# Feed-forward operands: the parts of the second quarter ahead of the last quarter's scaling and of the second difference

## The chip, the cores and the metric

The kernel runs on one core of a Trainium2 chip. The metric is the device time of one execution in microseconds, lower is better. Engines: TensorE (PE in the profile) multiplies, VectorE (DVE), ScalarE (ACT) and GpSimd (POOL) work elementwise, SyncE (SP) issues DMAs; ScalarE issues some too. Each takes its instructions from its own queue in program order and waits on semaphores that the others increment.

## The reference

One layer of a hybrid decoder over 2048 prompt tokens and 32 sample tokens, all fp32. The part that matters here is the feed-forward and the embedding that the kernel computes ahead of it:

```python
def hybrid_layer(x, pe, ...):
    ...
    x = x + jnp.concatenate([h_m, y_c], axis=-1) @ w_out
    f = rmsnorm(x, g_ffn)
    x = x + (jax.nn.silu(f @ w_gate) * (f @ w_up)) @ w_down
    e = rmsnorm(pe @ w_ple, g_ple)
    x = x + jax.nn.sigmoid(x @ w_pg) * e
```

The model width is 1024, the hidden width 2816. Ahead of this lie the input projection, an mLSTM with a recurrent state, and a short convolution.

## The kernel before

**Groups and stages.** Tokens are handled in three groups q of 704 (the last of 672, with the sample tokens). Each goes through the stages in, out, the embedding (ple), feed-forward (ffn) and pg, with all weights read anew. Activations lie with features on partitions; a group is cut into two halves of 352 (336) columns.

**Products.** A weight block of 1024 x 256 is multiplied as a 2 x 2 by 2 x 2 block product in Winograd's form, with 7 products in place of 8. Each of these runs over 4 blocks of 128 rows. fp32 accuracy comes from a split: every operand is held as a high part, rounded to fp32r, and a low part, the rest; `three` issues hi x hi, hi x lo and lo x hi. So a product is 12 matmuls of 352 columns. The order here is P1, P5, P2, P6, P7, P4, P3 (`FIRST_PRODUCTS`), and in feed-forward the first gate pair and the first up pair run as twins: P1 of gate, P1 of up, P5 of gate, P5 of up, and so on. These 14 products have the slots s = 0 to 13; hooks called `ffn_first` (one on ScalarE, one on VectorE) run behind slot s.

**Operands.** The moving operands of the stage are seven, made once for all pairs. With f the normed input, B11, B21 the upper and lower features of the first half, B12, B22 of the second:

- operand 0 is B11 (`R45`), read by P1; operand 4 is T1 = B12 - B11 (`mixq`), read by P5
- operand 1 is B21 (`mixr`), the second quarter, read by P2
- operand 2 is B22 (`qraw[:, 2]`), the last quarter, read by P3; it is made by a scaling with the norm's factors, `f_normed(q, 1, 1, ...)`
- operand 5 is the second difference T2 = B22 - T1 (`R67`), made by `t_sums(q, "ffn", 5)`, read by P6
- operand 6 is T2 - B11 (P7), operand 3 is B21 - T2 (P4), made by `t_sums` with 6 and 3

ScalarE makes the high part of an operand with one copy (`high_of`, line 1301), which waits until the operand is made. VectorE subtracts it from the operand for the low part (`low_of`, line 1778) and waits for the copy. For operand 2 GpSimd does that (its own `low_of`, line 2666), and waits for operand 5 to be made besides.

**Who does what around the twin pair.** `embedding` on each engine runs while TensorE multiplies the embedding: 16 small products k, each evicted by ScalarE (line 1540). VectorE makes operands 0, 4, 1, 2 and 5 there. In the twin pair each engine calls `product` per slot, and ahead of its own work `ahead()`, which prepares one weight entry further on: ScalarE rounds it (line 1283) and GpSimd subtracts (line 2652), for the entry four products ahead; VectorE forms the weight sums S1 to S4. In the second and third group most entries are loaded from DRAM instead, where the first group stored them; ScalarE issues these loads in `ahead()`. An entry lies in one of five ring slots and may be overwritten once its product is done.

On ScalarE a slot is `ahead()`, then for P1 and P2 the eviction of the bank, then the hook. On VectorE a slot is `ahead()`, then the sum that takes in the bank of this product (line 1889 for P6, lines 1894 and 1897 or 1899 to 1904 for P7, 1911 for up's P2), then the hook. P6 and P7 of a pair use the same bank, so P7 starts only when line 1889 is done.

SyncE loads the raw weights of a block (`raw`) as soon as the last weight entry of the block two before has its low part, in one of two buffers `wraw`.

In the table of counters the low parts are waited for in this order, one semaphore for 0 to 6 and another (`low2`) for operand 2:

```python
def highs(q, st):
    ...
    return 0, 4, 1, 5, 6, 3, 2
```

Of the kernel before, what the change touches and what calls it, by code (L numbers as in the profile page):

```python
# [58 lines left out]
def sources(q, st):  # L59

    if st == "in":
        return 0, 1, B12, 2, 4, 5, 3, 6
    return {"out": (0, 4, 5, 6, 3), "ffn": (0, 4, 1, 2, 5, 6, 3), "pg": (4, 5, 6, 3)}[st]


def highs(q, st):

    if st == "in":
        return (0, B12, 1, 2, 4, 5, 3, 6) if q else (0, 1, B12, 2, 4, 5, 3, 6)
    return 0, 4, 1, 5, 6, 3, 2  # L70


def slot(i):

    return 6 if i == B12 else i
# [90 lines left out]
def build(nc, x_prompt, x_sample, p_prompt, p_sample, state_C, state_n, state_m, state_conv, g_mix, w_in,  # L166
# [129 lines left out]
    def source(q, st, i):  # L296
        if i in (3, 6) or st == "pg" and i == 5:
            return qraw[:, i, :, 0:q.N]
        c = q.blocks
        if st in ("in", "out"):  # L300
            a = q.A if st == "in" else q.U
            if i == 5:
                return qraw[:, 5, :, 0:q.N] if st == "in" else Rz[:, :, 0:q.N]
            return {0: a[:, 0:4, c[0]], B12: a[:, 0:4, c[1]], 4: a[:, 0:4, c[1]], 1: a[:, 4:8, c[0]], 2: a[:, 4:8, c[1]]}[i]
        if st == "ffn":
            return {0: R45, 4: mixq, 1: mixr, 2: qraw[:, 2], 5: R67}[i][:, :, 0:q.N]
        return {0: q.X[:, 0:4, c[0]], 1: q.X[:, 4:8, c[0]], 2: q.X[:, 4:8, c[1]], 4: diff[:, :, 0:q.N]}[i]
# [190 lines left out]
    def freed(q, st, i):  # L498

        if st == "in" and i == 6:  # L500
            return operand_end[(q, "in", B12)]
        if st == "in" and q == 0:
            return None
        return operand_end[(q - (st == "in"), BEFORE[st], slot(i))]

    with ExitStack() as ctx:
# [744 lines left out]
        def _(act):  # L1251
# [33 lines left out]
            def ahead():  # L1285

                one_ahead()
                if n_hi[0] < len(entries) and entries[n_hi[0]].spare is not None:
                    one_ahead()

            def high_of(q, st, i):

                if i in sources(q.n, st):
                    act.wait_ge(src_ready, SOURCE[(q.n, st, i)])
                elif st == "out":
                    act.wait_ge(gated, 6 * q.n + (5 if i == 1 else 6))
                else:
                    act.wait_ge(x3, 16 * q.n + (7, 15, 16)[i])
                if freed(q.n, st, i):
                    act.wait_ge(prod, freed(q.n, st, i))  # L1300
                nc.scalar.activation(qhi[:, slot(i), :, 0:q.N], source(q, st, i), ACT.Copy).then_inc(high, 1)
# [228 lines left out]
                return after  # L1530

            def embedding(q):
                for k in range(16):
                    if k % 4 == 0:
                        ahead()
                    if k == 1:
                        res_square(q, 3)
                    act.wait_ge(*written[(q.n, "ple", k)])
                    bk = 6 + k % 2
                    nc.scalar.activation(q.U[:, k // 2, q.blocks[k % 2]], bank[bk][:, 0:q.N], ACT.Copy).then_inc(free[bk], 1)  # L1540
                    if k in (10, 13):
                        high_of(q, "ffn", {10: 0, 13: 4}[k])
# [22 lines left out]
            def silu_part(q, c, b, name):  # L1565
                act.wait_ge(*drained[(q.n, "gate", 0, name)])
                nc.scalar.activation(sl[:, c, q.blocks[b]], sl[:, c, q.blocks[b]], ACT.Silu).then_inc(silu_done, 1)

            def ffn_first(q):
                def after(s):  # L1570
                    if s in (0, 2, 4, 6, 8):
                        high_of(q, "ffn", highs(q.n, "ffn")[2 + s // 2])
                    if s == 8:
                        silu_part(q, 1, 1, "P5")
                    if s == 10:
                        silu_part(q, 1, 0, "P4")
                    if s == 12:
                        silu_part(q, 0, 1, "P3")
                    if s == 13:
                        hidden_high(q, 0, 1)  # L1580
                return after
# [56 lines left out]
            q = supers[0]  # L1638
# [65 lines left out]
            q = supers[2]  # L1704
# [5 lines left out]
        def _(dve):  # L1710
# [65 lines left out]
            def low_of(q, st, i):  # L1776
                dve.wait_ge(high, HIGH[(q.n, st, i)])
                nc.vector.tensor_tensor(qlo[:, slot(i), :, 0:q.N], source(q, st, i), qhi[:, slot(i), :, 0:q.N], sub)\  # L1778
                    .then_inc(low2 if i == 2 else low, 1)

            def made(q, st, *which):

                dve.wait_ge(src_ready, max(SOURCE[(q.n, st, i)] for i in which))

            def free_operand(q, st, i):
                if freed(q.n, st, i):
                    dve.wait_ge(prod, freed(q.n, st, i))
# [572 lines left out]
            def embedding(q):  # L2360
                for k in range(3):
                    ahead()
                    if k == 0:
                        res_add(q, 3)
                mean_squares(q, "res", 5, res_mean, 2 * (q.n + 1))
                f_normed(q, 0, 0, R45).then_inc(src_ready, 1)
                link(f_normed(q, 0, 1, mixq))
                made(q, "ffn", 0)
                nc.vector.tensor_tensor(mixq[:, :, 0:q.N], mixq[:, :, 0:q.N], R45[:, :, 0:q.N], sub).then_inc(src_ready, 1)
                low_of(q, "ffn", 0)  # L2370
                ahead()
                f_normed(q, 1, 0, mixr).then_inc(src_ready, 1)
                made(q, "ffn", 1)
                dve.sem_inc(free[3], 1)
                low_of(q, "ffn", 4)
                free_operand(q, "ffn", 2)
                f_normed(q, 1, 1, qraw[:, 2]).then_inc(src_ready, 1)
                made(q, "ffn", 2)
                dve.sem_inc(free[4], 1)
                t_sums(q, "ffn", 5)  # L2380
# [29 lines left out]

            def ffn_first(q):
                def after(s):
                    if s in (0, 2, 4, 6):
                        low_of(q, "ffn", (1, 5, 6, 3)[s // 2])
                    if s in (0, 2):
                        t_sums(q, "ffn", (6, 3)[s // 2])
                    if s == 13:
                        hidden_low(q, 0, 1)
                return after
# [115 lines left out]
            q = supers[0]  # L2535
# [63 lines left out]
            q = supers[2]  # L2599
# [8 lines left out]
        def _(pool):  # L2608
# [52 lines left out]
            def low_of(q, st):  # L2661

                pool.wait_ge(high, HIGH[(q.n, st, 2)])
                if st == "ffn":
                    pool.wait_ge(src_ready, SOURCE[(q.n, "ffn", 5)])
                nc.gpsimd.tensor_tensor(qlo[:, 2, :, 0:q.N], source(q, st, 2), qhi[:, 2, :, 0:q.N], ALU.subtract).then_inc(low2, 1)
# [147 lines left out]
            for q in supers:  # L2814
                plain_pair(q, in_after(q))
                ahead()
                ahead()
                for i in range(1, IN_PAIRS):
                    pair(in_after(q), 7 * i)
                for j in range(14):  # L2820
                    ahead()
                    if j == 8:
                        low_of(q, "out")
                for i in range(2, 4):
                    pair(nothing, 0)
                for k in range(4):
                    ahead()
                    if k == 1:
                        inverse_means(q, res_mean, res_root)
                for p in range(FFP):  # L2830
                    if p == 0:
                        for j in range(14):
                            ahead()
                            if j == 9:
                                low_of(q, "ffn")
                        continue
                    pair(nothing, 0)
                    if down_before(p) is not None:
                        for k in range(8 if down_before(p) else 4):
                            ahead()  # L2840
                    if p == 1:
                        for k in range(5):
                            ahead()
                        inverse_means(q, e_mean, e_root)
                        ahead()
                        ahead()
                    else:
                        pair(nothing, 0)
                for k in range(8):
                    ahead()  # L2850
                for i in range(4):
                    pair(pg_after(q), 7 * i)

            q = supers[2]
# [28 lines left out]
```

## Time and profile before

| | |
|---|---|
| median of 3 runs | 2640.02 us (2639.51 to 2642.21) |
| the profiled execution | 2641.59 us, its span 2639.9 us |
| TensorE busy | 2504.7 us, 95% of the span |
| VectorE busy | 1487.6 us, 56% |
| GpSimd busy | 1054.5 us, 40% |
| ScalarE busy | 908.1 us, 34% |
| mean granted clock of TensorE | 0.978 of full |

The profile is of one execution. Busy times are sums over instructions; a gap of TensorE is read in its timeline, where the bracket says how long it stood idle and which instruction ended that. "issue" there means that no releaser shows. Line numbers are those of the kernel before. The three groups' feed-forward starts lie at about 368, 1250 and 2103 us.

### The profile page before, as it was taken

Reading aid. Unit: us, or ns where it says so; the run is one execution under the profiler, and the core shown is the slowest. Engines: PE = TensorE matmul, PEld = TensorE weight load, DVE = VectorE, ACT = ScalarE, POOL = GpSimd, SP = SyncE. Lnnn points to the kernel's source line nnn. Section 1 sums busy time; section 2 is a strip of 40 time slices with the busy share of each in tenths; the row PEclk is TensorE's granted clock in tenths of the full one; section 3 lists DMA queues with packets and bytes.
Section 4 is the critical chain, followed back from the end, with each engine's and each line's share of the span. In section 5 each row is a group of like instructions: output and inputs, shape, how many; then the busy total and the mean of one; then the engine's idle time right before and its main releaser. Section 6 shows DMA issues by size and latency. Waiting matters only on the chain.

```text
span 2639.9 us, 41288 instructions
## 1 busy us (share of the span) xinstructions
PE 2504.7 (95%) x15883; PEld 2442.7 (93%) x15883; DVE 1487.6 (56%) x2283; ACT 908.1 (34%) x1687; POOL 1054.5 (40%) x864
## 2 busy tenths in 40 slices
PE   7998888999999999999999999998999999999997
PEld 6898778999999988999999999998899999999997
DVE  6667877765555674466643333467347664333355
ACT  5344443343333542333322121354134432212133
POOL 4566645676666343222332122334223232312233
PEclk8999888999999999999999999999999999999999
DMA  5556635576566746565555545575557555564544
GB/s 185 201 182 225 213 113 178 205 267 218 201 224 236 232 143 193 175 230 176 188 172 200 171 150 174 176 236 161 182 173 230 189 195 167 192 200 160 174 146 162
DMA packets 285046, 501.04 MB, mean 190 GB/s; under 512 B 18427, under 2 KB 182612, under 8 KB 284342
## 3 DMA queue, kind: packets, MB, share of 16 engines
q1 hardware_dynamic: 212182, 273.59, 30.8%
q10 hardware_dynamic: 72672, 224.82, 26.0%
q8 instruction: 129, 2.11, 0.3%
q14 instruction: 63, 0.52, 0.1%
HBM read 374.70 MB, written 123.65 MB: 189 GB/s over the span
## 4 chain that ended last, share of the span: by engine, by line
PE 69%; DVE 8%; DMA 6%; issue 3%; POOL 3%; ACT 1%; DVEq 0%; POOLq 0%; ACTq 0%
PE bank L603 22%; PE bank L605 21%; PE bank L604 21%; POOL wring L2652 3%; DMA wring<-weight_parts 2%; DMA weight_parts<-wring 2%; DVE qlo L1778 1%; PE bank L726 1%; DMA xs<-x_prompt 1%; PE bank L737 1%; DVE sg L2513 0%; PE bank L789 0%; PE bank L795 0%; ACT wring L1283 0%; DVE wraw L1768 0%
## 5 line engine op out<-in xcount | busy, mean ns | idle before, releaser
L2652 POOL TENSOR_TENSOR wring<-wraw,wring 128x512 fp32r<-128x512 f32 x531 | 785.3, 1488 | 1232.8 <-ACT wring L1283 1230.0
L603 PE MATMUL bank<-qhi,wring 128*128 128x352 f32 (+1 forms) x3588 | 1175.6, 328 | 72.7 <-DVE u L1832 14.9
L605 PE MATMUL bank<-qhi,wring 128*128 128x352 f32 (+1 forms) x3588 | 1157.2, 323 | 0.0
L604 PE MATMUL bank<-qlo,wring 128*128 128x352 f32 (+1 forms) x3588 | 1156.3, 322 | 0.0
L603 PEld LDWEIGHTS bank<-qhi,wring 128*128 128x128 f32 x3588 | 684.9, 191 | 98.9 <-issue 80.6
L604 PEld LDWEIGHTS bank<-qlo,wring 128*128 128x128 f32 x3588 | 684.5, 191 | 0.0
L605 PEld LDWEIGHTS bank<-qhi,wring 128*128 128x128 f32 x3588 | 682.3, 190 | 0.0
L1283 ACT ACTIVATE wring<-wraw 128x512 fp32r<-128x512 f32 x531 | 331.4, 628 | 734.8 <-PE bank L605 549.1
L603 PE MATMUL bank<-hid,wring 128*128 128x352 f32 (+1 forms) x1056 | 340.5, 322 | 11.2 <-DVE wide L2472 6.1
L605 PE MATMUL bank<-hid,wring 128*128 128x352 f32 (+1 forms) x1056 | 339.3, 321 | 0.0
L604 PE MATMUL bank<-hid,wring 128*128 128x352 f32 (+1 forms) x1056 | 338.4, 320 | 0.0
L2472 DVE TENSOR_TENSOR wide<-wide,bank 128x352 f32<-128x352 f32 (+1 forms) x288 | 148.1, 515 | 293.1 <-PE bank L605 293.1
L603 PEld LDWEIGHTS bank<-hid,wring 128*128 128x128 f32 x1056 | 199.5, 189 | 15.2 <-issue 11.6
L604 PEld LDWEIGHTS bank<-hid,wring 128*128 128x128 f32 x1056 | 200.1, 189 | 0.0
L605 PEld LDWEIGHTS bank<-hid,wring 128*128 128x128 f32 x1056 | 199.3, 189 | 0.0
L1839 DVE TENSOR_TENSOR u<-t,bank 128x352 f32<-128x352 f32 (+1 forms) x84 | 43.2, 514 | 189.0 <-PE bank L605 188.9
L2652 POOL TENSOR_TENSOR wring<-s,wring 128x512 fp32r<-128x512 f32 x74 | 107.8, 1468 | 69.0 <-ACT wring L1283 68.5
L1832 DVE TENSOR_TENSOR u<-t,bank 128x352 f32<-128x352 f32 (+1 forms) x87 | 44.6, 512 | 139.5 <-PE bank L605 110.9
L1563 ACT ACTIVATE hid<-sl 128x704 fp32r<-128x704 f32 (+3 forms) x69 | 52.1, 755 | 186.6 <-DVE sl L1810 181.0
L2406 DVE TENSOR_TENSOR hid<-sl,hid 128x704 fp32r<-128x704 f32 (+3 forms) x69 | 102.5, 1496 | 9.2 <-ACT hid L1563 7.5
L1312 ACT ACTIVATE t<-bank 128x352 f32<-128x352 f32 (+1 forms) x123 | 56.3, 457 | 135.9 <-PE bank L605 135.7
L1283 ACT ACTIVATE wring<-s 128x512 fp32r<-128x512 f32 x74 | 45.7, 628 | 91.2 <-PE bank L605 52.3
(318 smaller groups left out, 2468.7 us busy)
## 6 DMA issues: line engine op xcount, KB each, us to landing
wring<-weight_parts ACTq DMA_DIRECT2D x418, 512.0 KB, 4.5
weight_parts<-wring SPq DMA_DIRECT2D x201, 512.0 KB, 3.9
wraw<-w_down SPq DMA_DIRECT2D x33, 1024.0 KB, 7.1
wraw<-w_in SPq DMA_DIRECT2D x14, 1024.0 KB, 6.7
wraw<-w_gate SPq DMA_DIRECT2D x11, 1024.0 KB, 6.0
wraw<-w_up SPq DMA_DIRECT2D x11, 1024.0 KB, 6.1
wraw<-w_in SPq DMA_DIRECT2D x44, 256.0 KB, 4.3
wraw<-w_gate SPq DMA_DIRECT2D x44, 256.0 KB, 4.2
```

What stands on the lines that cost most here:

```text
L603: nc.tensor.matmul(o, hi, mh, start=begins, stop=False, skip_group_check=True)
L604: nc.tensor.matmul(o, hi, ml, start=False, stop=False, skip_group_check=True)
L605: return nc.tensor.matmul(o, lo, mh, start=False, stop=ends, skip_group_check=True)
L726: last = nc.tensor.transpose(bank[bk][0:n, c * P:(c + 1) * P], q.X[:, m * 4 + c, t0:t0 + n], ident[:, :])
L1283: nc.scalar.activation(whi[e % RING][:, :].rearrange("p (k n) -> p k n", k=k), w.src, ACT.Copy).then_inc(hi_done, 1)
L1312: nc.scalar.activation(t1[n % 2][:, 0:q.N], bank[a][:, 0:q.N], ACT.Copy).then_inc(free[a], 1)
L1563: nc.scalar.activation(hid[:, 0, x, blk], sl[:, c, blk], ACT.Copy).then_inc(h_hi, 1)
L1832: nc.vector.tensor_tensor(w2, t, c, add).then_inc(fc, 1)
L1839: nc.vector.tensor_tensor(w3, w2 if first else t, d, add).then_inc(fd, 1)
L2406: nc.vector.tensor_tensor(hid[:, 1, x, blk], sl[:, c, blk], hid[:, 0, x, blk], sub).then_inc(h_lo, 1)
L2472: last = nc.vector.tensor_tensor(x, x, bank[bk][:, 0:q.N], add)
L2652: nc.gpsimd.tensor_tensor(wlo[e % RING][:, :].rearrange(v, k=k), w.src, whi[e % RING][:, :].rearrange(v, k=k), ALU.subtract).then_inc(lo_d ...
```

## The change

On ScalarE the copy for the high part of operand 1 moves from the hook of slot 0 to the end of `embedding`, behind its last eviction, and the copies of operands 5, 6, 3 and 2 move from slots 2, 4, 6, 8 to 0, 2, 4, 6. On VectorE the low part of operand 1 moves from slot 0 to `embedding`, ahead of the scaling that makes operand 2 and of the second difference; the low parts of 5, 6 and 3 move from slots 2, 4, 6 to 0, 2, 4. The sums that make operands 6 and 3 keep their slots 0 and 2, behind the low part in the same slot. On GpSimd the low part of operand 2 moves from behind the tenth to behind the eighth weight entry of the twin pair.

```diff
             def embedding(q):
-                for k in range(16):
+                for k in range(17):
+                    if k == 16:
+                        high_of(q, "ffn", 1)
+                        break
                     if k % 4 == 0:
                         ahead()
...
             def ffn_first(q):
                 def after(s):
-                    if s in (0, 2, 4, 6, 8):
-                        high_of(q, "ffn", highs(q.n, "ffn")[2 + s // 2])
+                    if s in (0, 2, 4, 6):
+                        high_of(q, "ffn", highs(q.n, "ffn")[3 + s // 2])
...
                 low_of(q, "ffn", 4)
+                low_of(q, "ffn", 1)
                 free_operand(q, "ffn", 2)
                 f_normed(q, 1, 1, qraw[:, 2]).then_inc(src_ready, 1)
...
             def ffn_first(q):
                 def after(s):
-                    if s in (0, 2, 4, 6):
-                        low_of(q, "ffn", (1, 5, 6, 3)[s // 2])
+                    if s in (0, 2, 4):
+                        low_of(q, "ffn", (5, 6, 3)[s // 2])
                     if s in (0, 2):
                         t_sums(q, "ffn", (6, 3)[s // 2])
...
                         for j in range(14):
                             ahead()
-                            if j == 9:
+                            if j == 7:
                                 low_of(q, "ffn")
```

## Rows read from the trace of the kernel before

**Rows 1.** View by stretches, the three twin pairs: busy us (xcount) by engine

```profile
368.50:408.80 40.30, 32.11 (x170) 31.07 (x169) 36.07 (x35) 18.00 (x27) 23.59 (x14) 0.87 0.43 157
1250.20:1277.90 27.70, 27.04 (x168) 26.50 (x167) 21.77 (x24) 14.19 (x19) 12.35 (x5) 1.00 0.64 226
2103.10:2129.70 26.60, 25.97 (x170) 25.71 (x169) 21.05 (x25) 13.77 (x20) 11.99 (x5) 1.00 0.66 230
```

**Rows 2.** TensorE's timeline at its gaps: start, us, instruction, [idle before <-releaser]

```profile
379.32 0.63 PE L603 MATMUL bank<-qhi,wring 128*128 128x352 f32 x1 [2.47 <-issue]
...
393.77 0.63 PE L603 MATMUL bank<-qhi,wring 128*128 128x352 f32 x1 [5.01 <-DVE u L1889]
...
404.91 0.40 PE L603 MATMUL bank<-qhi,wring 128*128 128x352 f32 x1 [0.52 <-issue]
...
418.48 0.63 PE L603 MATMUL bank<-qhi,wring 128*128 128x352 f32 x1 [3.79 <-DVE u L1832]
...
1258.39 0.40 PE L603 MATMUL bank<-qhi,wring 128*128 128x352 f32 x1 [0.55 <-issue]
...
2110.97 0.39 PE L603 MATMUL bank<-qhi,wring 128*128 128x336 f32 x1 [0.63 <-issue]
```

**Rows 3.** Timeline of VectorE, second group

```profile
1248.09 2.05 DVE L2356 SCALAR_TENSOR_TENSOR mixr<-wide,gains,bank 128x352 f32<-128x352 f32 x4
...
1254.02 1.62 DVE L2008 TENSOR_TENSOR R<-qraw,mixq 128x1408 f32<-128x1408 f32 x1
1255.56 2.72 DVE L1778 TENSOR_TENSOR qlo<-mixr,qhi 128x1408 fp32r<-128x1408 f32 x1
1258.21 1.61 DVE L2012 TENSOR_TENSOR qraw<-R,R 128x1408 f32<-128x1408 f32 x1
...
1264.79 0.51 DVE L1889 TENSOR_TENSOR u<-t,bank 128x352 f32<-128x352 f32 x1
1265.22 1.85 DVE L1778 TENSOR_TENSOR qlo<-qraw,qhi 128x1408 fp32r<-128x1408 f32 x1
```

**Rows 4.** Timeline of ScalarE, second group

```profile
1249.91 0.81 ACT L1540 ACTIVATE wide<-bank 128x352 f32<-128x352 f32 x2
...
1252.48 1.38 ACT L1301 ACTIVATE qhi<-mixr 128x1408 fp32r<-128x1408 f32 x1
1253.75 0.63 ACT L1283 ACTIVATE wring<-wraw 128x512 fp32r<-128x512 f32 x1
...
1254.27 0.46 ACT L1312 ACTIVATE t<-bank 128x352 f32<-128x352 f32 x1
1255.68 1.38 ACT L1301 ACTIVATE qhi<-R 128x1408 fp32r<-128x1408 f32 x1 [0.95 <-DVE R L2008]
```

**Rows 5.** Timeline of VectorE, first group

```profile
374.81 2.27 DVE L2008 TENSOR_TENSOR R<-qraw,mixq 128x1408 f32<-128x1408 f32 x1
...
393.12 0.51 DVE L1889 TENSOR_TENSOR u<-t,bank 128x352 f32<-128x352 f32 x1
...
400.17 1.55 DVE L1752 TENSOR_TENSOR s<-wraw 128x512 f32<-128x512 f32 x1 [1.42 <-DMA wraw<-w_gate]
```

**Rows 6.** Timeline of GpSimd, first and second group

```profile
386.82 7.50 POOL L2652 TENSOR_TENSOR wring<-wraw,wring 128x512 fp32r<-128x512 f32 x4 [1.10 <-ACT wring L1283]
...
401.12 3.69 POOL L2666 TENSOR_TENSOR qlo<-qraw,qhi 128x1408 fp32r<-128x1408 f32 x1
...
1254.45 2.35 POOL L2652 TENSOR_TENSOR wring<-wraw,wring 128x512 fp32r<-128x512 f32 x1 [1.38 <-ACT wring L1283]
```

**Rows 7.** Timeline of SyncE's queue, first group

```profile
394.35 0.38 SPq L1069 DMA_DIRECT2D wraw<-w_gate  x1
```

**Rows 8.** The page's DMA issues: KB each, median us to landing

```profile
wring<-weight_parts ACTq DMA_DIRECT2D x418, 512.0 KB, 4.5
```

**Rows 9.** View by stretches, behind gaps of 1.81 and 1.77 us

```profile
1295.00:1303.00 8.00, 7.73 (x48) 7.73 (x49) 4.21 (x9) 0.00 (x0) 0.00 (x0) 1.00 0.53 142
2147.00:2152.00 5.00, 5.00 (x24) 4.99 (x24) 1.57 (x4) 0.00 (x0) 0.00 (x0) 0.66 0.52 152
```

## The prediction

> **What bounds the kernel now.** I first cut the run into stretches and took the three feed-forward starts, one per group of tokens [rows 1]. TensorE is busy for 27.04 of 27.70 us in the second group and 25.97 of 26.60 in the third, at full clock; in the first group only for 32.11 of 40.30, clock 0.87. So TensorE sets the pace and what I look for are its gaps. Its own timeline then gives them [rows 2]: in the first group 2.47 us ahead of P2 of the gate (at 379.32; it needs the low part of operand 1), 5.01 ahead of P7 (at 393.77; released by VectorE's line 1889, the sum that empties the bank of P6), 0.52 ahead of P3 (404.91; operand 2's low part) and 3.79 in the next pair. In the second and third group the only gap up to the end of the twin pair is that ahead of P2: 0.55 and 0.63 us. VectorE's timeline of the second group [rows 3] shows why: it works through one list without a pause. ScalarE's timeline [rows 4] shows the rounding copies (line 1301) between its own evictions and weight preparations.
>
> **What the order of the code does to the queues.** I write low(i) and high(i) for the parts of operand i, s for the slot after each product. ScalarE executes slot s of the twin pair as: prepare the weights of product s+4, evict, then the hook. Each hook's high(i) waits until operand i is made, and everything behind it in ScalarE's queue waits too. Before, high(1) sits in slot 0 and is ready at once; high(5) in slot 2 (1252.48 and 1255.68 [rows 4]). After, high(5) moves to slot 0, high(6) to slot 2, high(3) to slot 4, high(2) to slot 6. On VectorE low(1) goes ahead of the scaling of operand 2 and of T2, and low(5), low(6), low(3) each move two slots forward. Nothing is added or removed: the same copies, subtractions and loads. But two couplings change. First, low(3) (1.85 us at 1265.22) ran behind the sum of line 1889 (1264.79) and now runs ahead of it. Second, VectorE had always another subtraction between making an operand and needing its high part back: T2 made, then low(1) and T6, and only then low(5) [rows 3]. After, the order is T2, low(5), T6, low(6), T3, low(3): each low part needs a copy by ScalarE that can't start before the operation just ahead of it on VectorE. The copy of 1.38 us is no longer covered, three times over.
>
> **The second group, step by step.** mixr is made at 1250.14 (1248.09 plus 2.05); ScalarE has finished its two evictions at 1250.7, so high(1) runs 1250.6 to 1252.0 and low(1) 1252.0 to 1253.6 at the 1.62 of an undisturbed subtraction. Scaling of operand 2 (2.05) and T2 (1.62, with 0.14 between as now) end at 1257.45 instead of 1255.64: +1.8. From there, each subtraction by its spacing (four of them and the short sum of line 1911, 0.44, fill 1258.21 to 1264.79: 1.54 each; 1.6 behind a wait) and each copy by 1.38 with 0.05 of hand-over: high(5) to 1258.9, low(5) 1260.5, T6 1262.05, high(6) 1263.5, low(6) 1265.1, T3 1266.65, high(3) 1268.1, low(3) 1269.7, the up pair's P2 sum 1270.1, line 1889 1270.6. P7 of the gate starts 0.14 later (393.12 plus 0.51 against 393.77 in the first group [rows 2, 5]): 1270.75. It started four products behind P2 of the gate: 1258.39 + 48 matmuls of 0.16 (27.04 us for 168 [rows 1]) = 1266.1. So +4.65 where no subtraction is disturbed.
> A subtraction of VectorE beside one of GpSimd took 2.72 instead of 1.62 (low(1) at 1255.56 [rows 3] beside the weight's low part at 1254.45, which took 2.35 [rows 6]). Up to three of the list can meet one (weights of P2, of up P2, of P4): 0 to 3.3 more. I take 1.0, as GpSimd is on in 12.35 of 27.7 us [rows 1] and in some meetings it is GpSimd that gets longer: +5.6 in all, between 4.0 and 8.
> The Trainium skill (SBUF — State Buffer, section Who interferes with whom) says that a VectorE operation with two SBUF inputs and a GpSimd operation that reads SBUF take turns, the second one waiting until the first is done. The trace's 2.72 agrees. By that rule in full, three meetings of a whole GpSimd subtraction would make the step some 8; without it, 4.65.
> What the early low(1) gives: P2 of the gate starts without its 0.55. But the up pair's P2 then waits: its weights are prepared and the bank of its P1 evicted (1253.75 and 1254.27 [rows 4]) behind high(5) now, thus at 1259 to 1260, and GpSimd's low part (1.3 to 2.4 us) ends near 1261.7, where it began at 1260.3. P6 and P6 of up wait likewise, for weights whose loads ScalarE issues only behind high(5) and high(6); a load lands 4.5 us after its issue in the median [rows 8]. Near 1264.5 and 1268.2 they start, against 1262.3 and 1264.2. All of this ends at about 1270.2, still ahead of line 1889, so it adds nothing: it is cover, and would take over if the list were shorter. Behind P7 nothing is early enough to be pinned elsewhere: sums, bank releases and the loads behind the Silu all follow P7, so the delay stays to the end.
>
> **The third group** is the same with 336 for 352 columns, so every term times 0.954: P7, which started at 2110.97 + 48 matmuls of 0.154 = 2118.4 [rows 1, 2], comes 4.4 later, with 0.95 for meetings 5.3, between 3.7 and 7.6.
>
> **The first group** also forms weight sums on VectorE. T2 ended at 377.08 [rows 5]; with low(1) ahead near 378.3. The sums S3 are now covered by waits for high(6), S4 is not. With the medium length of each subtraction I get low(5) 381.9, T6 383.7, high(6) 385.1, low(6) 387.6, T3 389.2, high(3) 390.6, low(3) 392.8, S4 of the gate 394.5, line 1889 396.7: P7 +3 (0.8 to 5.5). In exchange P2 of the gate starts 2.47 earlier, which up P2 gives back waiting for weights until about 381.8. Then the queue of GpSimd: its low(2) (3.69 us, at 401.12 [rows 6]) moves from slot 9 to slot 7, ahead of the weight of slot 8, the last of this gate's raw matrix. That weight's low part ended at 394.3, when SP issued the load of the next w_gate (394.35 [rows 7]), and VectorE's first sum of it began when it landed, at 400.17 [rows 5]. After: high(2) near 393, the weights of slots 5 to 7 to 396, low(2) to 399.7, slot 8 to 401.3, the load to 407. That is +6.7 for a list on VectorE that runs from 400.17 to the release at 418.48 [rows 2, 5]. With fewer meetings behind it I take +6.0, between 3 and 8; the 0.52 ahead of P3 goes, within it.
>
> **The clock.** A gap of 1.77 us in the third group is followed by a stretch at 0.66 of full clock over 5 us, i.e. the lower level of 1.2 GHz for 3.4 of them: 1.7 lost. After a gap of 1.81 us in the second group it stays at 1.00 [rows 9]. The second and third group get four gaps of 6 us in sum within 13 us. Where P7 and what follows run at the lower level, 1.5 to 1.7 is lost; I take 1.2 for each, between 0 and 1.7.
>
> **Sum.** 6.0 + 5.6 + 5.3 + 2.4 = 19.3 us. Against the profiled run of 2641.6 this is 2660.9; that run is 1.6 above the median, so 2659.3.
>
> **Rivals.** (a) The early operand keeps its worth: the three gaps ahead of P2 go (2.47 + 0.55 + 0.63), and the lower clock behind the first (about 1.4), with the 0.52 of P3: 5.6 faster, 2634.4. This needs line 1889 done by 1265.5 in the second group, thus the list from T2 in 8 us; four subtractions alone take 6.5, and three copies would have to be hidden. Against it speaks that each copy reads what was made just before. (b) The delay of P7 comes, but is taken up later: the 3.79 of the next pair in the first group and gaps of 1.8 in each of the others (1295.27 is one) absorb it. 19.3 less 7.4 is 11.9: 2651.9. Against it: those gaps too end with VectorE, which is late as well. (c) Only the operands' order counts and GpSimd's move is hidden: first group +3, 2656.3. (d) The lower clock covers most of the twin pair in the second and third group and meetings come thrice: 8 + 7.6 + 3.4 + 8, 27 slower: 2667. (e) It does nothing measurable, since TensorE waits elsewhere: nothing in the profile speaks for it.
>
> **How the numbers follow.** My case with (c), within 2651 to 2666: 7 in 10. (b): 0.14. (d): 0.09. (a): 0.04, (e): 0.03. The range goes from 2648 (all low ends: 3 + 4.0 + 3.7, less 2 for some of (b)) to 2667 and leaves out less than 2 in 10. Within 0.2% (5.3 us) of before, about what a measurement of this kernel can tell from no change, lies only (e): 0.03. Faster by more than that is (a): 0.04. Slower is the rest, 0.93.
>
> **What would show it.** In the profile after: ScalarE's copy of R (operand 5) directly ahead of the weight preparation that up P2 waits for; VectorE with three idle times of about 1.4 us ahead of line 1778, released by ScalarE; low(3) ahead of line 1889; the gap ahead of P7 in all three groups, released by line 1889, and P7 about 3, 5.6 and 5.3 later; the w_gate load of the first group issued near 401. I would be wrong if ScalarE's copies were found under other work of VectorE, or if TensorE's gaps from the following pair on shrank by what P7 was late.

## The result and the profile after

The changed kernel takes 2657.82 us (median of 5 runs, 2655.41 to 2661.39) against 2640.02 of before: ratio 1.0063, with an interval from 1.0051 to 1.0074. Slower by 17.8 us, clear of the noise. The forecast was 2659.3, from 2648 to 2667.

To see where, I measure each group between two marks that VectorE sets: its scaling of the means ahead of the feed-forward (line 2346 before, 2349 after) and the same line for the embedding's means, behind the second pair. Before, the three stretches are 109.95, 86.00 and 84.36 us; after, 116.07, 92.07 and 90.11. That is 6.1 + 6.1 + 5.8 = 17.9 us, all of the difference. In the page of the profile, TensorE has no more work than before (2498.8 us against 2504.7, and the same number of instructions), while the span has grown by 17.7:

```profile
span 2657.6 us, 41288 instructions
...
PE 2498.8 (94%) x15883; PEld 2434.8 (92%) x15883; DVE 1490.6 (56%) x2283; ACT 907.4 (34%) x1687; POOL 1054.4 (40%) x864
```

TensorE's timeline at its gaps, to be read beside [rows 2]:

```profile
380.67 0.57 PE L603 MATMUL bank<-qhi,wring 128*128 128x352 f32 x1 [3.41 <-POOL wring L2656]
...
396.66 0.63 PE L603 MATMUL bank<-qhi,wring 128*128 128x352 f32 x1 [8.43 <-DVE u L1892]
...
409.92 0.40 PE L603 MATMUL bank<-qhi,wring 128*128 128x352 f32 x1 [1.31 <-DVE bank L1903]
...
424.42 0.63 PE L603 MATMUL bank<-qhi,wring 128*128 128x352 f32 x1 [5.44 <-DVE u L1835]
...
1266.30 0.43 PE L603 MATMUL bank<-qhi,wring 128*128 128x352 f32 x1 [1.86 <-POOL wring L2656]
...
1271.52 0.43 PE L603 MATMUL bank<-qhi,wring 128*128 128x352 f32 x1 [1.13 <-DMA wring<-weight_parts]
...
1276.41 0.40 PE L603 MATMUL bank<-qhi,wring 128*128 128x352 f32 x1 [2.71 <-DVE u L1892]
...
1286.54 0.43 PE L603 MATMUL bank<-qhi,wring 128*128 128x352 f32 x1 [0.35 <-DMA wring<-weight_parts]
...
2126.79 0.42 PE L603 MATMUL bank<-qhi,wring 128*128 128x336 f32 x1 [1.86 <-POOL wring L2656]
...
2131.78 0.42 PE L603 MATMUL bank<-qhi,wring 128*128 128x336 f32 x1 [1.03 <-DMA wring<-weight_parts]
...
2136.50 0.39 PE L603 MATMUL bank<-qhi,wring 128*128 128x336 f32 x1 [2.60 <-DVE u L1892]
...
2147.32 0.42 PE L603 MATMUL bank<-qhi,wring 128*128 128x336 f32 x1 [1.37 <-DMA wring<-weight_parts]
```

The gap ahead of P2 of the gate is gone in all groups. Up P2 now waits (1.86 us in the second and third group, 3.41 in the first) for a weight's low part. Up P6 waits for a load (1.13 in the second group, 1.03 in the third). P7 waits for line 1892 (1889 before): 2.71 in the second group, 2.60 in the third and 8.43 in the first, in place of 0, 0 and 5.01. In the first group the 0.52 ahead of P3 of the gate is gone, but up P3 now waits 1.31 for a sum of VectorE (the row at 409.92). VectorE's timeline of the second group shows why, in place of [rows 3]:

```profile
1252.80 2.05 DVE L2359 SCALAR_TENSOR_TENSOR mixr<-wide,gains,bank 128x352 f32<-128x352 f32 x4
...
1256.69 1.62 DVE L1781 TENSOR_TENSOR qlo<-mixr,qhi 128x1408 fp32r<-128x1408 f32 x1
...
1260.43 1.62 DVE L2011 TENSOR_TENSOR R<-qraw,mixq 128x1408 f32<-128x1408 f32 x1
1263.50 1.62 DVE L1781 TENSOR_TENSOR qlo<-R,qhi 128x1408 fp32r<-128x1408 f32 x1 [1.45 <-ACT qhi L1301]
1265.04 2.68 DVE L2015 TENSOR_TENSOR qraw<-R,R 128x1408 f32<-128x1408 f32 x1
1269.17 1.62 DVE L1781 TENSOR_TENSOR qlo<-qraw,qhi 128x1408 fp32r<-128x1408 f32 x1 [1.45 <-ACT qhi L1301]
1270.72 1.62 DVE L2019 TENSOR_TENSOR qraw<-mixr,R 128x1408 f32<-128x1408 f32 x1
1273.78 1.62 DVE L1781 TENSOR_TENSOR qlo<-qraw,qhi 128x1408 fp32r<-128x1408 f32 x1 [1.45 <-ACT qhi L1301]
...
1275.75 0.95 DVE L1892 TENSOR_TENSOR u<-t,bank 128x352 f32<-128x352 f32 x2
```

Where there was no pause there are three of 1.45 us, each released by ScalarE's line 1301, and low(3), the row at 1273.78, is ahead of the sums of line 1892 (two rows merged at 1275.75). ScalarE, in place of [rows 4]:

```profile
1255.27 1.39 ACT L1301 ACTIVATE qhi<-mixr 128x1408 fp32r<-128x1408 f32 x1
...
1262.09 1.38 ACT L1301 ACTIVATE qhi<-R 128x1408 fp32r<-128x1408 f32 x1 [4.56 <-DVE R L2011]
...
1263.38 0.61 ACT L1283 ACTIVATE wring<-wraw 128x512 fp32r<-128x512 f32 x1
1263.89 0.45 ACT L1312 ACTIVATE t<-bank 128x352 f32<-128x352 f32 x1
1267.76 1.38 ACT L1301 ACTIVATE qhi<-qraw 128x1408 fp32r<-128x1408 f32 x1 [3.42 <-DVE qraw L2015]
...
1272.37 1.38 ACT L1301 ACTIVATE qhi<-qraw 128x1408 fp32r<-128x1408 f32 x1 [1.45 <-DVE qraw L2019]
```

ScalarE stands idle for 4.56 us until T2 is made, copies operand 5 (1262.09), and only then comes to the weight preparation (1263.38) and the eviction (1263.89) that up P2 needs.

The first group, by GpSimd, SyncE and VectorE, in place of [rows 5 to 7]:

```profile
397.17 3.20 POOL L2670 TENSOR_TENSOR qlo<-qraw,qhi 128x1408 fp32r<-128x1408 f32 x1
400.33 1.28 POOL L2656 TENSOR_TENSOR wring<-wraw,wring 128x512 fp32r<-128x512 f32 x1
```

```profile
401.63 0.38 SPq L1069 DMA_DIRECT2D wraw<-w_gate  x1
```

```profile
408.08 0.69 DVE L1755 TENSOR_TENSOR s<-wraw 128x512 f32<-128x512 f32 x1 [6.46 <-DMA wraw<-w_gate]
```

low(2) runs at 397.17, ahead of the weight at 400.33; only then is w_gate issued, at 401.63, and VectorE stands idle for 6.46 us until it lands. Counted from the marks (352.35 and 352.74), the load is issued 49.3 us in, where it was 41.6 before.

### The profile page after: what moved, and what is told of

Read it like the earlier page. It is cut to its first block, busy times and chain, and to the rows that moved or that the text cites. A ratio compares the mean times of both kernels' runs of the same rounds, so it can differ in the third digit from the quotient of the medians.

```text
span 2657.6 us, 41288 instructions
## 1 busy us (share of the span) xinstructions
PE 2498.8 (94%) x15883; PEld 2434.8 (92%) x15883; DVE 1490.6 (56%) x2283; ACT 907.4 (34%) x1687; POOL 1054.4 (40%) x864
## 4 chain that ended last, share of the span: by engine, by line
PE 65%; DVE 9%; DMA 7%; POOL 4%; issue 4%; ACT 2%; DVEq 0%; POOLq 0%; ACTq 0%; SPq 0%
PE bank L603 20%; PE bank L605 20%; PE bank L604 20%; POOL wring L2656 3%; DMA weight_parts<-wring 3%; DMA wring<-weight_parts 2%; DVE qlo L1781 1%; ACT qhi L1301 1%; PE bank L726 1%; PE bank L737 1%; DVE sg L2517 0%; PE bank L789 0%; ACT wring L1283 0%; DVE ess L2393 0%; DMA xs<-x_prompt 0%
## 5 line engine op out<-in xcount | busy, mean ns | idle before, releaser
L603 PEld LDWEIGHTS bank<-hid,wring 128*128 128x128 f32 x1056 | 198.9, 188 | 16.3 <-issue 12.5
```

The source lines that it names most:

```text
L603: nc.tensor.matmul(o, hi, mh, start=begins, stop=False, skip_group_check=True)
```

## The experiments

All times are medians, with the ratio to the kernel before that ran on the same chip. Beside these experiments single executions of the kernel before went from 2632 to 2647 us, so a difference of a few us between two experiments is weak by the medians; the stretches and gaps of the profiles show more. A profile is of one execution, though, and that one can lie far from its median: e6's is the slowest of its runs, e4's, e8's and e10's are among the fastest. The column "profiled" gives its time. The last column is TensorE's time lost to the lower clock in the second and third stretch (1 less the granted clock, times the time, summed over pieces of 2 us). The first stretch loses 10 to 16 us in every profile (13.3 before, 14.2 changed).

| kernel | median us | ratio (interval) | profiled | 1st stretch | 2nd | 3rd | lost 2nd, 3rd |
|---|---|---|---|---|---|---|---|
| before | 2640.0 | 1 | 2641.6 | 109.95 | 86.00 | 84.36 | 0, 1.7 |
| changed | 2657.8 | 1.0063 (1.0051 to 1.0074) | 2659.3 | 116.07 | 92.07 | 90.11 | 0, 0 |
| e1 early only | 2639.7 | 0.9994 (0.9984 to 1.0004) | 2640.0 | 110.44 | 87.29 | 84.52 | 1.7, 1.7 |
| e2 GpSimd back | 2658.7 | 1.0073 (1.0055 to 1.0091) | 2660.5 | 115.82 | 93.14 | 89.74 | 3.4, 1.7 |
| e3 low(3) back | 2655.0 | 1.0051 (1.0036 to 1.0067) | 2654.2 | 116.65 | 91.07 | 87.42 | 0, 1.7 |
| e4 copies covered | 2651.9 | 1.0045 (1.0031 to 1.0058) | 2646.2 | 114.68 | 89.46 | 86.42 | 1.7, 1.7 |
| e5 shift only | 2660.4 | 1.0082 (1.0064 to 1.0099) | 2659.8 | 115.08 | 92.68 | 89.92 | 3.4, 3.4 |
| e6 ScalarE a slot later | 2657.8 | 1.0069 (1.0049 to 1.0089) | 2667.9 | 115.01 | 94.52 | 90.57 | 5.1, 3.4 |
| e7 low(3) back, covered | 2655.2 | 1.0057 (1.0040 to 1.0074) | 2658.0 | 114.10 | 91.52 | 87.51 | 3.4, 1.7 |
| e8 every repair | 2641.0 | 1.0003 (0.9990 to 1.0016) | 2636.0 | 109.44 | 88.06 | 82.60 | 1.7, 0 |
| e9 e8, low(3) ahead | 2645.7 | 1.0022 (1.0013 to 1.0031) | 2645.7 | 109.62 | 89.79 | 83.61 | 1.7, 0 |
| e10 e8, copies open | 2649.8 | 1.0035 (1.0021 to 1.0049) | 2644.2 | 110.45 | 88.40 | 86.74 | 0, 0 |
| e11 e8, GpSimd early | 2647.5 | 1.0023 (1.0011 to 1.0034) | 2642.2 | 112.67 | 86.15 | 83.22 | 0, 0 |

**Is it the early operand or the shift of the others?** e1 keeps the first and undoes the second; e5 does the reverse.

```diff
# e1, against the changed kernel
-                    if s in (0, 2, 4, 6):
-                        high_of(q, "ffn", highs(q.n, "ffn")[3 + s // 2])
+                    if s in (2, 4, 6, 8):
+                        high_of(q, "ffn", highs(q.n, "ffn")[2 + s // 2])
...
-                    if s in (0, 2, 4):
-                        low_of(q, "ffn", (5, 6, 3)[s // 2])
+                    if s in (2, 4, 6):
+                        low_of(q, "ffn", (5, 6, 3)[s // 2 - 1])
...
-                            if j == 7:
+                            if j == 9:
```

> Against the changed kernel, only the early copy and subtraction of operand 1 stay; operands 5, 6, 3, 2 and GpSimd's subtraction return to their old slots. Theory of the prediction (the cost comes from the two-slot shift, not from the early operand): low(3) is again behind the sum that frees P6's bank and each copy of ScalarE is covered by another operation of VectorE, so P7 is on time; the gap ahead of gate P2 goes. 2638.5 us, between 2636 and 2641. Rival (the early low part itself costs, since T2 ends 1.8 us later in each group): 1 to 2 us slower per group than before, 2643 to 2646.

Measured 2639.7, ratio 0.9994: no different from before. The early operand costs nothing; it doesn't bring anything either. The gap ahead of gate P2 is gone in all groups, but in the first group TensorE then stands for 4.51 us ahead of gate P6 (the row below), since VectorE's list is no shorter; in the third it waits 0.50 us for a load right behind the twin pair.

```profile
387.68 0.40 PE L603 MATMUL bank<-qhi,wring 128*128 128x352 f32 x1 [4.51 <-issue]
```

```diff
# e5, against the changed kernel
-                for k in range(17):
-                    if k == 16:
-                        high_of(q, "ffn", 1)
-                        break
+                for k in range(16):
...
             def ffn_first(q):
                 def after(s):
+                    if s == 0:
+                        high_of(q, "ffn", 1)
                     if s in (0, 2, 4, 6):
...
-                low_of(q, "ffn", 1)
                 free_operand(q, "ffn", 2)
...
             def ffn_first(q):
                 def after(s):
+                    if s == 0:
+                        low_of(q, "ffn", 1)
                     if s in (0, 2, 4):
```

> The changed kernel with operand 1's copy and subtraction back in slot 0 (low(1) ahead of low(5)), the two-slot shift of 5, 6, 3 and 2 kept. Theory: T2 ends 1.8 us earlier, low(1) covers the copy of operand 5, and of the three idle times of VectorE two stay, as does low(3) ahead of the sum that frees P6's bank: P7 3.9 and 3.7 us later than before in the second and third group, some 4.6 in the first: 2652, between 2649 and 2655. Rival 1 (the early low(1) is what costs): 2640 to 2643. Rival 2 (the early low(1) costs nothing, all comes from the shift): 2657.

Measured 2660.4, ratio 1.0082, above the expected range: rival 2 by the time. In the second group P7 (the row below) starts 33.10 us behind the mark; before it was 1266.1 - 1236.94 = 29.2. So it is 3.9 late, as worked out, not 5.6. The rest of these two stretches is clock: this profile loses 3.4 us in the second and third each, the changed kernel's none. In the first group P7 is only 2.1 late, and the stretch 5.1 longer: w_gate lands 7.0 later from the mark than before. The shift alone makes the whole loss, though not by P7's delay alone.

```profile
1272.29 0.63 PE L603 MATMUL bank<-qhi,wring 128*128 128x352 f32 x1 [2.84 <-DVE u L1891]
```

**Which coupling of the shift?** e3 moves low(3) back behind the sum, e4 covers two copies, e6 takes ScalarE's copies off up P2's weights.

```diff
# e3, against the changed kernel
-                    if s in (0, 2, 4):
-                        low_of(q, "ffn", (5, 6, 3)[s // 2])
+                    if s in (0, 2, 6):
+                        low_of(q, "ffn", {0: 5, 2: 6, 6: 3}[s])
```

> The changed kernel with VectorE's low(3) alone back in slot 6, behind the sum that frees P6's bank. Theory: P7 of the gate comes earlier by low(3) and the idle time ahead of it, 1.54 + 1.45 = 3.0 us in each group; in the second and third group that stays to the end; in the first it does not, since the load of w_gate waits for GpSimd's queue (weights of slots 5 to 7, then low(2)), which starts from the copy of operand 3 and is not moved. So 6 us less than the changed kernel: 2652. Rival 1 (the place of low(3) is the whole cost): 5.6 less per group, near 2641. Rival 2 (copies without cover are the whole cost and low(3) is not): 2657.

Measured 2655.0, 2.9 less than the changed kernel where 6 were worked out; by the times alone rival 2 is not excluded (the intervals overlap), the stretches give 1.0 and 2.7 less in the second and third group. In the first group nothing is gained, as expected. The next fence is TensorE's timeline of e3 in the second group: no wait for line 1892 is left ahead of P7, but four of the weight path are, two of them new, ahead of up P7 and right behind the twin pair.

```profile
1266.73 0.43 PE L603 MATMUL bank<-qhi,wring 128*128 128x352 f32 x1 [1.94 <-POOL wring L2656]
...
1271.84 0.43 PE L603 MATMUL bank<-qhi,wring 128*128 128x352 f32 x1 [0.99 <-DMA wring<-weight_parts]
...
1276.58 0.43 PE L603 MATMUL bank<-qhi,wring 128*128 128x352 f32 x1 [0.65 <-DMA wring<-weight_parts]
...
1287.80 0.43 PE L603 MATMUL bank<-qhi,wring 128*128 128x352 f32 x1 [1.29 <-DMA wring<-weight_parts]
```

```diff
# e4, against the changed kernel
-                    if s in (0, 2, 4):
-                        low_of(q, "ffn", (5, 6, 3)[s // 2])
                     if s in (0, 2):
                         t_sums(q, "ffn", (6, 3)[s // 2])
+                    if s in (0, 2, 4):
+                        low_of(q, "ffn", (5, 6, 3)[s // 2])
```

> The changed kernel with VectorE's order inside slots 0 and 2 turned round: T6 ahead of low(5), T3 ahead of low(6), so that ScalarE's copies of 5 and 6 lie under a subtraction. low(3) stays ahead of the sum that frees P6's bank. Theory: the three idle times of VectorE (1.45 each) go, the list ends 4.3 us earlier; TensorE is then held by up P2's weights and starts P7 near 4.1 us earlier than in the changed kernel in the second and third group, 3 in the first: 2646.5, between 2644 and 2650. Rival (the place of low(3) is what costs): no more than 1 us less than the changed kernel, 2656 to 2658.

Measured 2651.9 (2645.6 to 2655.0), 6 less than the changed kernel where 11 were worked out. P7 waits for no sum in the second and third group. The stretches, of a profiled run at 2646.2, gain 1.4, 2.6 and 3.7. The open copies are thus a part of the cost, and by these figures a larger one than low(3) (e9 and e10 below show each alone); the rival is out.

```diff
# e6, against the changed kernel
-                    if s in (0, 2, 4, 6):
+                    if s in (1, 3, 5, 7):
                         high_of(q, "ffn", highs(q.n, "ffn")[3 + s // 2])
```

> The changed kernel with ScalarE's copies of 5, 6, 3, 2 one slot later (1, 3, 5, 7), thus behind the eviction and the weight preparation that up P2 waits for. Theory: up P2, P6 and up P6 start earlier, their gaps go, the gap ahead of P7 grows by as much, the time stays: 2657.8, within 1.5. Rival (the late weights of up P2, P6 and up P6, 1.9 + 1.1 us per group of gaps, are the cost): 3 us less per group, 2649.

Measured 2657.8, as expected, no different from the changed kernel. The gaps of up P2 and up P6 are gone in the second group, and the one ahead of P7 has nearly their sum (5.29 us, for 1.86 + 1.13 + 2.71; first fence: TensorE's timeline of e6). P7 did start a little earlier from the mark, by 0.7 to 0.9 us in each group, but this profile, of the slowest run (2667.9), lost 8.5 us to the clock in the second and third stretch. The second fence is its view by stretches behind that gap.

```profile
1277.95 0.63 PE L603 MATMUL bank<-qhi,wring 128*128 128x352 f32 x1 [5.29 <-DVE u L1892]
```

```profile
1277.90:1283.90 6.00, 5.95 (x23) 5.99 (x24) 1.38 (x3) 0.50 (x1) 4.55 (x3) 0.57 0.71 196
```

e7 joins e3 and e4: both repairs of VectorE's list, with ScalarE's order and GpSimd's left as in the changed kernel.

```diff
# e7, against the changed kernel
-                    if s in (0, 2, 4):
-                        low_of(q, "ffn", (5, 6, 3)[s // 2])
                     if s in (0, 2):
                         t_sums(q, "ffn", (6, 3)[s // 2])
+                    if s in (0, 2, 6):
+                        low_of(q, "ffn", {0: 5, 2: 6, 6: 3}[s])
```

> The changed kernel with both repairs of VectorE's order: T6 ahead of low(5), T3 ahead of low(6), and low(3) behind the sum that frees P6's bank. ScalarE's order and GpSimd's stay. Theory: VectorE no longer holds P7 in the second and third group; what stays is the wait of up P2 for weights behind the copy of operand 5 (2.0 us, against the 0.55 of before), thus +1.5 to 2 per group, and in the first group GpSimd's queue ahead of the w_gate load, +3: 2646, between 2643 and 2649.

Measured 2655.2, far more than expected. No gap for line 1892 is left in the second and third group; the wait of up P2 is (2.06 us in each), and loads that up P3 waits for add 0.40 and 1.05. Right behind the wait of up P2 the lower clock takes 1.7 more, 1.6 of it in the row below (view by stretches of e7, from the gap at 1266.34 on):

```profile
1266.00:1270.40 4.40, 4.06 (x16) 4.07 (x17) 3.82 (x3) 3.44 (x5) 0.43 (x2) 0.64 0.92 313
```

**Everything repaired, and then each cost by itself.**

```diff
# e8, against e7
-                    if s in (0, 2, 4, 6):
+                    if s in (1, 3, 5, 7):
                         high_of(q, "ffn", highs(q.n, "ffn")[3 + s // 2])
...
-                            if j == 7:
+                            if j == 8:
```

> As the run before, and ScalarE's copies of 5, 6, 3, 2 one slot later (1, 3, 5, 7) so that up P2's weights are not behind them, and GpSimd's low(2) behind the ninth weight, so that it is ahead neither of the last weight of the gate matrix nor behind the Silu. Theory: every cost found is gone, the gap ahead of gate P2 too; no gap above 0.5 us up to P7 in the second and third group; first group as before or 1 us shorter. 2638, between 2635 and 2640.5. Rival (moving these parts at all costs, by meetings of VectorE and GpSimd): 2643 or more.

Measured 2641.0, ratio 1.0003, just above the expected range. All of the loss is undone, and nothing is won. VectorE's list in the second group of e8 has no pause, as before the change (first fence). TensorE waits 0.59 us for a load ahead of up P3 instead (second fence):

```profile
1246.88 1.77 DVE L2011 TENSOR_TENSOR R<-qraw,mixq 128x1408 f32<-128x1408 f32 x1
1248.76 1.62 DVE L2015 TENSOR_TENSOR qraw<-R,R 128x1408 f32<-128x1408 f32 x1
1250.30 1.62 DVE L1781 TENSOR_TENSOR qlo<-R,qhi 128x1408 fp32r<-128x1408 f32 x1
1251.84 1.62 DVE L2019 TENSOR_TENSOR qraw<-mixr,R 128x1408 f32<-128x1408 f32 x1
1253.38 1.62 DVE L1781 TENSOR_TENSOR qlo<-qraw,qhi 128x1408 fp32r<-128x1408 f32 x1
...
1255.34 0.51 DVE L1892 TENSOR_TENSOR u<-t,bank 128x352 f32<-128x352 f32 x1
1255.77 2.47 DVE L1781 TENSOR_TENSOR qlo<-qraw,qhi 128x1408 fp32r<-128x1408 f32 x1
```

```profile
1267.27 0.43 PE L603 MATMUL bank<-qhi,wring 128*128 128x352 f32 x1 [0.59 <-DMA wring<-weight_parts]
```

```diff
# e9, against e8
-                    if s in (0, 2, 6):
-                        low_of(q, "ffn", {0: 5, 2: 6, 6: 3}[s])
+                    if s in (0, 2, 4):
+                        low_of(q, "ffn", (5, 6, 3)[s // 2])
# e10, against e8: low_of of 5, 6 and 3 in the same slots, but ahead of t_sums
# e11, against e8
-                            if j == 8:
+                            if j == 7:
```

> The kernel with every repair, but with low(3) again in slot 4, ahead of the sum that frees P6's bank; the copies stay covered. Theory: VectorE's list to that sum grows by one subtraction without idle time; P7 of the gate 1.1 to 1.7 us later than before in the second and third group, 2 in the first, plus 1.7 where the clock falls: 2645, between 2643 and 2648. Rival (low(3) is free where the copies are covered): 2641.

> The kernel with every repair, but with low(5) again ahead of T6 and low(6) ahead of T3, so that two copies of ScalarE lie open; low(3) stays behind the sum that frees P6's bank. Theory: two idle times of 1.45 us on VectorE ahead of that sum, P7 of the gate 2.4 us later than before in the second and third group, 1.5 in the first, plus 1.7 where the clock falls: 2647, between 2644 and 2650. Rival (the open copies lie under TensorE's own work as long as low(3) is behind): 2641.

> The kernel with every repair, but with GpSimd's low(2) behind the eighth weight in place of the ninth, thus ahead of the last weight of the first gate matrix in the first group. Theory: the load of w_gate is issued 3.2 us later and VectorE's list behind it ends 3 us later; the first group's stretch 112.5 us against 109.4; second and third unchanged: 2644. Rival (as putting it back in the changed kernel showed, the move is hidden or paid by a meeting elsewhere): 2641.

e9: 2645.7, as expected; the gap ahead of P7 is 0.91 and 0.78. e10: 2649.8, upper end of the range; the gaps are 2.23 and 2.18 by the expected two idle times of VectorE. The times alone set only e10 apart from e8, with intervals that do not overlap; for e9 and e11 what tells is the gaps and stretches. The rows of e9 and e10 in the second group, TensorE's of e9 and of e10, then VectorE's of e10:

```profile
1267.02 0.40 PE L603 MATMUL bank<-qhi,wring 128*128 128x352 f32 x1 [0.91 <-DVE u L1892]
```

```profile
1266.99 0.40 PE L603 MATMUL bank<-qhi,wring 128*128 128x352 f32 x1 [2.23 <-DVE u L1892]
```

```profile
1258.21 1.63 DVE L1781 TENSOR_TENSOR qlo<-R,qhi 128x1408 fp32r<-128x1408 f32 x1 [1.45 <-ACT qhi L1301]
...
1262.82 1.63 DVE L1781 TENSOR_TENSOR qlo<-qraw,qhi 128x1408 fp32r<-128x1408 f32 x1 [1.45 <-ACT qhi L1301]
```

e11: 2647.5 (expected 2644); the first stretch is 112.67, 3.2 more than in e8, as worked out, and the rest of the 6.5 by the medians shows in no stretch of its profile, which is of one of its shorter runs (2642.2). And e7 differs from e11 in ScalarE's slots alone: 7.8 us by the medians, with intervals that do not overlap, and 1.4 + 5.4 + 4.3 = 11.1 by the stretches. Of these 11.1, 5.1 are e7's loss to the clock in the second and third stretch, where e11 lost none; some 6 are the order itself, 2 a group. So ScalarE's order is a full cost by itself, but hidden where VectorE's list is longer (e6).

Last, GpSimd's move in the changed kernel:

```diff
# e2, against the changed kernel
-                            if j == 7:
+                            if j == 9:
```

> The changed kernel with GpSimd's low(2) alone back behind the tenth weight of the twin pair. Theory: in the first group the last weight of the gate matrix no longer waits 3.2 us behind low(2) in GpSimd's queue, so SyncE issues the load of w_gate near 398.4 in place of 401.6 and the list of VectorE behind it ends 3 us earlier; nothing changes in the second and third group. First group's stretch 113 us in place of 116.1, the kernel 2655. Rival (that move is hidden): all three stretches as in the changed kernel, 2657.8.

Measured 2658.7, the rival. SyncE does issue w_gate at 397.71, near what was worked out, and it lands 2.8 us earlier from the mark, but low(2) now runs beside VectorE's first sum of it, which takes 2.95 us in place of 0.69, and the first stretch is 115.82 against 116.07. Even so the load is issued 397.71 - 351.16 = 46.6 us behind the mark, 4.9 later than before the change. So of its delay of 7.7 us GpSimd's move makes 2.7, and the rest is there without it. GpSimd, SyncE and VectorE of e2:

```profile
403.24 3.23 POOL L2670 TENSOR_TENSOR qlo<-qraw,qhi 128x1408 fp32r<-128x1408 f32 x1
```

```profile
397.71 0.38 SPq L1069 DMA_DIRECT2D wraw<-w_gate  x1
```

```profile
404.06 2.95 DVE L1755 TENSOR_TENSOR s<-wraw 128x512 f32<-128x512 f32 x1 [3.20 <-DMA wraw<-w_gate]
```

## Why the prediction held, step by step

The time (2657.8 against 2659.3) and the range were right, and so was the cause: the shift of operands 5, 6, 3 and 2, not the early operand. That the sum came within 1.5 us is in part luck: the term of the clock did not appear in the profile and small gaps that the forecast left out took its place, and in the first group two errors of some 1.5 us cancel.

- **VectorE's list, second and third group.** T2 forecast 1.8 us later against mixr, measured (1262.05 - 1252.80) - (1255.64 - 1248.09) = 1.7. P7 forecast +5.6 and +5.3, measured (1276.41 - 1252.80) - (1266.1 - 1248.09) = 5.6, and 5.4 in the third group. Three idle times of 1.45 for the forecast 1.4; one meeting with GpSimd (2.68 for 1.62) for the 1.0 taken. e9 and e10 show the two couplings apart: 0.9 and 2.2 us of gap; together (e6) 5.3. They add up to more, since with low(3) ahead the third copy (1.45) lies open too, and since the slack of the list is used up only once: line 1892 starts 16.1 us behind mixr in e8, 19.0 in e10 and 22.0 in e6, so e10's gap of 2.2 comes from a list that is 2.9 longer.
- **The early operand.** Forecast as worth no more than its gap, given back at up P2. e1 shows that even where up P2 doesn't give it back the kernel is not faster.
- **"It is cover, and would take over if the list were shorter."** Right in kind: up P2 began 1266.30 - 1252.80 = 13.5 behind mixr, forecast 1261.7 - 1248.09 = 13.6, and e6 moved the gaps and not the time. Its size alone I had put at 1.5 to 2 us a group for e7; e7 against e11 gives 2.6 by the medians, and by the stretches 3.7 with the clock and 2.0 without. That this wait, with the loads behind it and the clock, took over is why e3, e4 and e7 gave back less than expected.
- **First group.** P7 forecast +3, measured (396.66 - 352.35) - (393.77 - 352.74) = 3.3, the last number of each bracket being the mark; w_gate's landing +6.7, measured (408.08 - 352.35) - (400.17 - 352.74) = 8.3; but VectorE's list behind it was 16.3 us in place of 18.3, where I had taken off 0.7. Sum 6.1 for 6.0, by two errors that cancel. The list is shorter because low(2) no longer meets it (two sums of 1.55 and 1.78 us before, 0.69 each after): e2 lands 2.8 earlier and loses 2.3 of it in that meeting. So GpSimd's move costs next to nothing here, and with the others repaired (e11) it costs its 3.2. That the 0.52 ahead of P3 goes was right, but up P3 waits 1.31 in its place.
- **"Behind P7 nothing is early enough to be pinned elsewhere."** Nearly: up P3's load is waited for, 0.35 us in the second group and 1.37 in the third.
- **The clock, 2.4 us.** This term failed in the profiled run: the granted clock stays at 1.00 through all the gaps of the second and third stretch (the fence below), and the third stretch even saves the 1.7 that before lost at 2147 [rows 9]. Other profiles with gaps of much the same size do lose it (e2, with 1.86 and 2.55 in the second group, loses 3.4 and 1.7; e5 3.4 and 3.4). Each is one execution of another kernel. The mean granted clock also differs between executions of one kernel (0.977 to 0.980 in the five of the changed kernel, and the profiled one has the highest), but where in the kernel the others lose it no profile shows. In the profiled run the load ahead of up P3 and 0.5 us more at the next gap of the third group (2.30 for 1.77) stand in its place.

View by stretches, the second and third stretch of the changed kernel:

```profile
1241.65:1333.72 92.07, 83.94 (x520) 82.02 (x521) 57.89 (x81) 33.58 (x48) 24.12 (x15) 1.00 0.48 157
2102.97:2193.08 90.11, 80.62 (x520) 78.72 (x521) 57.30 (x80) 32.64 (x48) 23.21 (x15) 1.00 0.49 162
```

Rival (b), a delay taken up later, is out: the gaps of the next pair stay (5.44 for 3.79; 1.73 for 1.81; 2.30 for 1.77). Rival (a) is out by the gaps ahead of P7. Of rival (c) one half holds and one does not: in the changed kernel GpSimd's move is hidden (e2), but the first group loses 6.1 and not 3, since w_gate is issued 4.9 late without it too. Rival (d) asked for the lower clock and three meetings a group; the profile has neither, and no run came above 2661.4. Rival (e) is out by the interval.

What is left is why e8 and e1, without the gap ahead of gate P2 (0.55 and 0.63 us, 2.47 in the first group), are not measurably faster than before. In the first group VectorE's list takes it back. In the second group of e8 a load ahead of up P3 takes 0.59 and the gap of the next pair grows from 1.81 to 2.26; in the third of e1 a load takes 0.50 and that gap grows from 1.77 to 2.30. For the third group of e8, which has no such load, it stays open: without the clock's part the stretch is 82.6 against 82.7, a difference that the runs can't tell from none. What decides when the lower clock comes stays open too.

## What to carry to other kernels

An operation that waits for a round trip to another engine (make, copy there, subtract here) should have another piece of the own list between the making and the wait; when such steps are moved ahead with nothing left between them, each becomes an open round trip (1.45 us of idle time here), and on the engine at the other end everything queued behind the waiting copy is late as well. Ask of every step moved forward which release of a bank now stands behind it. And repair all the waits of a stretch before judging one: two of them in parallel hide each other (e6 against the changed kernel showed nothing of the 7.8 us that e7 against e11 did).

## What was unexpected of the hardware

- The loss by the lower clock in the second and third stretch came in equal parts of 1.7 us (0, 1.7, 3.4 or 5.1 per stretch), and not in order of the gaps: none behind gaps of 1.86, 1.13 and 2.71 us in the changed kernel, 1.7 behind one of 2.06 in e7, 0.57 of full clock over 6 us behind one of 5.29 in e6.
- A sum of VectorE with both inputs in SBUF went from 0.69 to 2.95 us beside a subtraction of GpSimd of 3.23: more than a fourfold time for a short one. The sum began 0.8 us behind that subtraction and ended 0.5 behind its end. In the list one meeting cost 1.1. The Trainium skill (SBUF — State Buffer, section Who interferes with whom) has the second of two such operations wait until the first is done. The trace agrees for this one: by that rule the sum would take 3.23 - 0.82 + 0.69 = 3.1, and 2.95 were measured.
